# Three stretches reordered in a two-block transformer kernel: a gate unit's tiles, attention scores behind two tiles, and decays ahead of convolution terms

## The chip, the cores and the metric

The kernel runs on one core of a Trainium2 chip. Its engines work side by side, each through its own list of instructions in order: PE (TensorE, matrix products), ACT (ScalarE, functions of one operand and copies), DVE (VectorE, everything with two operands), POOL (GpSimd) and SP (SyncE, which here only starts transfers). They wait for each other by semaphores: an instruction adds to one when it is done, another waits until it has reached a value. The metric is the time of one execution on the device in microseconds (us), the median of several runs.

## The reference, cut to what matters

512 positions of 1024 float32 values go through two blocks.

```python
# first block
u = rmsnorm(h, ...); q, k, v, f, gate = split(u @ w_in_a)
h = h + (fox_attention(q, k, v, log_sigmoid(f)) * silu(gate)) @ w_out_a   # "first attention"
k_s, v_s = split(rmsnorm(h, kv_norm_g) @ w_kv)
q, gate = split(rmsnorm(h, norm_b_g) @ w_in_b)                            # 16 heads, 8 pairs
o = swa_sink_attention(rope(rmsnorm(q)), rope(rmsnorm(k_s)), v_s, sinks)  # window of 128
h = h + (o * silu(gate)) @ w_out_b                                        # "second attention"
# second block
(hq, hf, hi, hg, sq, sk, sv, iq, ik, iw, cu) = split(modulated_norm(x) @ w_in)
o_a = hgrn2_mixer(hq, hf, hi, hg)      # 4 heads: q * decays * k, chunks of 64, a state carried on
o_b = dsa_mixer(sq, sk, sv, iq, ik, iw)  # index scores pick 128 keys of each row, then softmax
o_c = conv_module(cu)                    # gated, causal depthwise filter of 31 taps, layer norm, silu
x = x + g1 * (concat([o_a, o_b, o_c]) @ w_out)
x = x + g2 * (square(relu(modulated_norm(x) @ mlp_w1)) @ mlp_w2)
return rmsnorm(x)
```

## The kernel before, in words

Everything is held transposed, features on the 128 partitions and the 512 positions along the row. A weight matrix is cut into units of 128 output columns. A unit comes in as 128 x 1024 float32 (`load_unit`), ACT rounds it to `wH` (L1936) and DVE or POOL subtracts that for the rest `wL` (L2442, L498). The product of a unit is 8 tiles of 128 input features with three matmuls each, L868 (high x high), L869 (high weight x low data) and L870 (low weight x high data), 24 matmuls of 128x512 into one bank `G`. They are `gemm(...)`, and a call may be given only some of the tiles, with other PE work in between. `FIRST` is tiles 0 to 3 and `SECOND` tiles 4 to 7. So the order in which PE works is written out by hand, in the block under `@block.tensor`, and so are those of ACT, DVE, POOL and SP.

Around the change there are three places.

**Second attention.** The loop over `n` (8 pairs of heads) interleaves, on PE, the query unit of pair n + 1 (`gemm_q`), the gate unit of pair n (`gemm_z`), scores in two halves (`scores_b(pe, n, 0)` and `(n, 1)`, L1214, L1216 and L1222, into the banks `S`), the turning of the exponentials (`turn_b`, L1269) and their product with the values (`mix_b`, L1285). `scores_b(n, 1)` writes over the banks from which ACT takes the exponentials of the first half (`exps_b`, L1249), so it waits for them. On ACT the second half of the sigmoid of the gate (`silu_scalar_2`, L887) waits for DVE (`silu_vector_1`, L882), and `take_turned_b` (L1277) and `widen_b` (L1296) feed `mix_b` and `spread_b` on PE.

**Selected attention.** DVE picks the keys with 16 rounds of MAX8 (L2758) and MATCH_REPLACE8 (L2759) for each block of rows, and between two rounds does other work (`between`), such as `logits_c` (L1115). PE meanwhile works off the input units of the second block (`gemm_i(n)`, unit UI + n) and six turns of scores (`scores_c(pe, k)`, L1103), which need queries and keys from unit 10 (`raw(10)` on ACT, L2141).

**The four heads of the recurrent mixer.** `window(t)` stands once on each engine, for head t of 0 to 3. PE makes the sums of logarithms (`diff(t, j)`, L1691) into two banks `S` in turn, ACT raises them (`decay(t, e)`, L2242, with e = j + 1), DVE multiplies them onto q and k (`operand`, L2793), PE multiplies these (`product`, L1709) and DVE gathers the results (`joined`, L2804). `diff(t, LV0 + 3)`, `LV0 + 4` and `LV0 + 5` each wait for a `joined` of DVE, because `half_of` puts products into the same banks. In windows 0 and 1 ACT also makes the terms of the depthwise filter (`conv_terms(slot)`, two terms, L2159, each into one of three buffers), and POOL adds them up (L533). A term waits until its buffer has been added. In windows 2 and 3 `conv_terms` does nothing.

Of the kernel before, what the change touches and what calls it, by code (L numbers as in the profile page):

```python
# [21 lines left out]
KT = D // P  # L22
# [146 lines left out]
def build(nc, a, out):  # L169
# [5 lines left out]
    with ctx:  # L175
# [52 lines left out]
        zraw, th = sb("zraw", [P, SEQ]), sb("th", [P, SEQ])  # L228
# [656 lines left out]
        def silu_scalar_2(act, ph, n, th):  # L885
            act.wait_ge(sem(f"{ph}_logsig"), n + 1 + since(f"{ph}_logsig"))
            s.activation(th, th, ACT.Exp).then_inc(sem(f"{ph}_sigmoid"), 1)  # L887
# [206 lines left out]
        def scores_c(pe, k):  # L1094
            t, r = C_TURNS[k]
            pe.wait_ge(sem("i_raw"), 11 + 2 * t)
            pe.wait_ge(sem("i_acc"), 24)
            for i, (q, at, w) in enumerate(A_ROUND[r]):
                for h in range(2):
                    if i == 0 and k:  # L1100
                        pe.wait_ge(sem("a_logits"), 64 + C_DONE[k - 1] + (h + 1) * (C_DONE[k] - C_DONE[k - 1]) // 2)
                    lo, hi = h * DH, (h + 1) * DH
                    last = mm(S[h][:, at:at + w], sqT[lo:hi, t, q * P:(q + 1) * P], skT[lo:hi, t, 0:w], start=(i == 0),  # L1103
                              stop=(i == len(A_ROUND[r]) - 1))
                    if i == len(A_ROUND[r]) - 1:
                        last.then_inc(sem("a_scores"), 1)
# [290 lines left out]
        def _(pe):  # L1397
# [157 lines left out]
            def gemm_z(n, part):  # L1555
                free = mark("b_raw", 1) if n == 0 else mark("b_raw", 8) if n == 7 else mark("b_zraw", n)
                gemm(pe, unit_z(n), hi2, lo2, free, part=part)
# [18 lines left out]
            for n in range(8):  # L1576
                if 0 < n < 7:
                    gemm_q(n + 1, FIRST)
                if n == 7:
                    gemm_z(n, range(2))  # L1580
                scores_b(pe, n, 0)
                if n:
                    turn_b(pe, n - 1, 1, 0)
                    turn_b(pe, n - 1, 1, 1)
                if 0 < n < 7:
                    gemm_q(n + 1, SECOND)
                if n == 7:
                    gemm_z(n, range(2, 6))
                if n:
                    mix_b(pe, n - 1, 1)  # L1590
                    spread_b(pe, n - 1)
                gemm_z(n, range(6, KT) if n == 7 else FIRST)
                scores_b(pe, n, 1)
                turn_b(pe, n, 0, 0)
                if n < 7:
                    sums_q(pe, n + 1)
                turn_b(pe, n, 0, 1)
                if n < 7:
                    gemm_z(n, SECOND)
                else:  # L1600
                    output_b(0, range(4))
                mix_b(pe, n, 0)
                if n < 7:
                    turn_q(pe, n + 1)
# [27 lines left out]
            def gemm_i(n, part=range(KT)):  # L1632
                gemm(pe, Unit(UI, n), hi2, lo2, mark("i_raw", n - 1), part=part)
# [221 lines left out]
            turn_sv(0)  # L1855
            turn_sv(1)
            gemm_i(10)
            scores_c(pe, 0)
            gemm_i(11)
            turn_c(pe, 0)  # L1860
            scores_c(pe, 1)
            gemm_i(12)
# [66 lines left out]
        def _(act):  # L1929
# [159 lines left out]
            for n in range(8):  # L2089
                if n:  # L2090
                    split_b(2 * n)
                    if n < 7:
                        silu_scalar_2(act, "b", n - 1, th[:, :])
                    take_turned_b(act, n - 1, 1)
                    widen_b(act, n - 1)
                    if n == 7:
                        silu_scalar_2(act, "b", n - 1, th[:, :])
                exps_b(act, n, 0)
                if 0 < n < 7:
                    take_q(act, n + 1)  # L2100
                if n:
                    gated_high(act, "b", n - 1, hi1)
                if n:
                    split_b(2 * n + 1)
                take_turned_b(act, n, 0)
                if n < 7:
                    root_scalar_q(act, link, n + 1)
                exps_b(act, n, 1)
                take_z(act, link, n)
# [187 lines left out]
            def take_hv(t):  # L2297
                act.wait_ge(sem("h_vturn"), t + 1 + since("h_vturn"))
                wait(act, sem("h_o"), t + since("h_o"))
                s.activation(vp[:, :, :], T[0][:, :].rearrange("p (c k) -> p c k", c=4), ACT.Copy).then_inc(sem("h_v"), 1)  # L2300
# [4 lines left out]
            def window(t):  # L2305
                def conv_terms(slot):
                    if t < 2 and 8 * t + slot < len(CONV_W) - 1:
                        terms(CONV_W[8 * t + slot], CONV_W[8 * t + slot + 1])
# [35 lines left out]
                if t == 2:  # L2344
                    act.wait_ge(sem("conv_sqsum"), 1)
                    rsqrt_scalar(link, 1, 1.0 / 256, sem("conv_var"), sem("conv_root"))
                conv_terms(2)
                decay(t, 5)
                take_hv(t)
                if t in (1, 3):  # L2350
                    root_h(t - 1)
                conv_terms(3)
# [733 lines left out]
```

## Time and profile before

| | |
|---|---|
| median of 3 runs | 1264.42 us (1263.88 to 1265.47) |
| the profiled execution | 1263.24 us, its span 1261.3 us |
| PE busy | 1247.8 us, 99% of the span |
| DVE, ACT, POOL busy | 696.7, 672.0, 370.9 us |
| mean granted TensorE clock | 0.997 |
| second attention's loop | from 375 us to 532 us |
| units of the second block's input and selected attention | from 580 us to 704 us |
| windows 0 to 3 | from 704 us to 855 us |

The span runs from the first instruction to the last; the time of the execution is 1.9 us longer. In the rows below a line of a timeline is: start, length, engine, line of the code, operation, output and inputs, shapes, how many merged into one, and in brackets how long the engine had been idle before it and what ended that. Engines overlap the end of one instruction with the start of the next, so lengths can add up to more than the distance of two starts.

### The profile page before, as it was taken

Reading aid. Unit: us, or ns where it says so; the run is one execution under the profiler, and the core shown is the slowest. Engines: PE = TensorE matmul, PEld = TensorE weight load, DVE = VectorE, ACT = ScalarE, POOL = GpSimd, SP = SyncE. Lnnn points to the kernel's source line nnn. Section 1 sums busy time; section 2 is a strip of 40 time slices with the busy share of each in tenths; the row PEclk is TensorE's granted clock in tenths of the full one; section 3 lists DMA queues with packets and bytes.
Section 4 is the critical chain, followed back from the end, with each engine's and each line's share of the span. In section 5 each row is a group of like instructions: output and inputs, shape, how many; then the busy total and the mean of one; then the engine's idle time right before and its main releaser. Section 6 shows DMA issues by size and latency. Waiting matters only on the chain.

```text
span 1261.3 us, 19235 instructions
## 1 busy us (share of the span) xinstructions
PE 1247.8 (99%) x7202; PEld 1004.7 (80%) x7202; DVE 696.7 (55%) x1477; ACT 672.0 (53%) x1278; POOL 370.9 (29%) x191
## 2 busy tenths in 40 slices
PE   9999999999999999999999999999999999999998
PEld 8777777778877777789676888888988888888887
DVE  6766667675575666565799546584662121121223
ACT  6666666666437676735667886753532242231331
POOL 0000000003410000053497784122255344353450
PEclk9999999999999999999999999999999999999999
DMA  5322243442333322252222022331363233232232
GB/s 197 112 68 84 84 145 123 134 135 96 105 101 101 101 84 85 84 176 84 84 85 71 29 70 68 118 134 47 105 217 116 70 115 101 84 107 94 84 100 68
DMA packets 38411, 128.11 MB, mean 102 GB/s; under 512 B 4640, under 2 KB 7584, under 8 KB 38320
## 3 DMA queue, kind: packets, MB, share of 16 engines
q1 hardware_dynamic: 35792, 121.91, 30.0%
q10 hardware_dynamic: 2528, 4.98, 1.2%
q8 instruction: 58, 0.95, 0.3%
q14 instruction: 33, 0.27, 0.1%
HBM read 123.43 MB, written 2.13 MB: 100 GB/s over the span
## 4 chain that ended last, share of the span: by engine, by line
PE 90%; issue 4%; DVE 2%; ACT 2%; POOL 1%; DMA 1%; ACTq 0%; DVEq 0%; POOLq 0%
PE G L868 21%; PE G L870 20%; PE G L869 20%; PE S L1691 2%; PE S L995 2%; PE O L1056 2%; PE T L1035 1%; PE S L1222 1%; PE T L1269 1%; PE O L1285 1%; PE S L1709 1%; PE N L1305 1%; PE N L1078 1%; PE N L1400 1%; PE N L1331 1%
## 5 line engine op out<-in xcount | busy, mean ns | idle before, releaser
L498 POOL TENSOR_TENSOR wL<-w,wH 128x1024 fp32r<-128x1024 f32 x119 | 290.9, 2449 | 833.9 <-ACT wH L1936 833.9
L868 PE MATMUL G<-hi,wH 128*128 128x512 f32 x1208 | 489.3, 405 | 0.8 <-DVE xT L963 0.4
L870 PE MATMUL G<-hi,wL 128*128 128x512 f32 x1208 | 472.0, 391 | 0.0
L869 PE MATMUL G<-lo,wH 128*128 128x512 f32 x1208 | 471.5, 390 | 0.0
L868 PEld LDWEIGHTS G<-hi,wH 128*128 128x128 f32 x1208 | 227.3, 188 | 58.0 <-issue 11.4
L1936 ACT ACTIVATE wH<-w 128x1024 fp32r<-128x1024 f32 x170 | 179.1, 1054 | 173.2 <-PE G L870 112.0
L870 PEld LDWEIGHTS G<-hi,wL 128*128 128x128 f32 x1208 | 227.0, 188 | 49.5
L869 PEld LDWEIGHTS G<-lo,wH 128*128 128x128 f32 x1208 | 227.7, 188 | 46.4 <-issue 3.1
L965 DVE SCALAR_TENSOR_TENSOR xT<-G,modT,xT 128x512 f32<-128x512 f32 x34 | 25.5, 751 | 124.5 <-PE G L870 124.4
L2414 ACT ACTIVATE tmp<-G 128x512 f32<-128x512 f32 x31 | 18.5, 598 | 118.4 <-PE G L870 114.8
L2442 DVE TENSOR_TENSOR wL<-w,wH 128x1024 fp32r<-128x1024 f32 x51 | 62.3, 1222 | 28.9 <-ACT wH L1936 28.0
L2965 DVE TENSOR_TENSOR T<-tmp,G 128x512 f32<-128x512 f32 x31 | 21.5, 695 | 94.4 <-ACT tmp L2414 94.4
L985 DVE CUSTOM_DVE_ANT_0 adaw<-adaw,scr 128x1024 f32<-128x1024 f32 x31 | 52.5, 1694 | 0.5 <-issue 0.4
L1023 ACT ACTIVATE scr<-scr,sa 128x256 f32<-128x256 f32 (+2 forms) x64 | 35.2, 557 | 26.9 <-DVE sa L1010 26.9
L2969 DVE TENSOR_TENSOR lo<-T,hi 128x512 fp32r<-128x512 f32 x32 | 22.1, 691 | 27.4 <-ACT hi L2421 27.4
L1249 ACT ACTIVATE scr<-S,bs,bq 128x128 f32<-128x128 f32 (+1 forms) x64 | 33.4, 536 | 3.6 <-DVE bs L1239 3.6
L2793 DVE TENSOR_TENSOR kd<-S,qkv 128x512 f32<-128x512 f32 x24 | 16.5, 689 | 30.3 <-ACT S L2242 27.7
L1046 ACT ACTIVATE scr<-T 128x384 f32<-128x384 f32 (+1 forms) x48 | 22.7, 525 | 12.0 <-PE T L1035 11.5
L1010 DVE CUSTOM_DVE_ANT_0 scr<-S,kd 128x256 f32<-128x256 f32 (+2 forms) x64 | 28.6, 487 | 0.0
L533 POOL TENSOR_TENSOR tmp<-tmp,rms 128x482 f32<-128x482 f32 (+19 forms) x20 | 24.4, 1220 | 11.2 <-ACT rms L2159 11.2
L2758 DVE MAX8 best<-adaw 128x8 f32<-128x256 f32 (+2 forms) x48 | 26.7, 557 | 0.8
L2759 DVE MATCH_REPLACE8 adaw<-best,adaw 128x256 f32<-128x256 f32 (+2 forms) x48 | 26.0, 543 | 0.0
(459 smaller groups left out, 1919.6 us busy)
## 6 DMA issues: line engine op xcount, KB each, us to landing
w<-weights_dram SPq DMA_DIRECT2D x170, 512.0 KB, 3.5
adaw<-ada_dram SPq DMA_DIRECT2D x43, 512.0 KB, 4.3
kd<-c_dram ACTq DMA_DIRECT2D x8, 512.0 KB, 3.7
cbias<-ada_dram SPq DMA_DIRECT2D x5, 512.0 KB, 4.5
xT<-x_dram SPq DMA_DIRECT2D x4, 512.0 KB, 7.9
out_dram<-xT SPq DMA_DIRECT2D x8, 256.0 KB, 2.6
scr<-ca_dram SPq DMA_DIRECT2D x2, 512.0 KB, 4.8
kd<-cbias SPq DMA_DIRECT2D x8, 128.0 KB, 3.2
```

The costliest lines, as they stand in the source:

```text
L498: g.tensor_tensor(wL[:, u.slot], w32[:, u.slot % 2], wH[:, u.slot].bitcast(f32), ALU.subtract).then_inc(w_lo, 1)
L868: mm(home[:, :], whi, H[:, k, :], start=(k == first), stop=False)
L869: mm(home[:, :], whi, L[:, k, :], start=False, stop=False)
L870: last = mm(home[:, :], wlo, H[:, k, :], start=False, stop=(k == final))
L985: v.tensor_tensor_reduce(out=home, in0=home, in1=copy, scale=1.0, scalar=0.0, op0=ALU.mult, op1=ALU.add, accum_out=modsum[:, b.n:b.n + 1]) ...
L1010: v.tensor_tensor_reduce(out=slot[:, h * 512 + at:h * 512 + at + w], in0=S[h][:, at:at + w], in1=kd[:, n % 2 * 2 + h, 0:w], scale=-1.0, sc ...
L1023: s.activation(part, part, ACT.Exp, bias=sa[:, n % 2, LOW, h, q:q + 1], scale=-1.0, accum_out=sa[:, n % 2, ASUM, h, q:q + 1]).then_inc(sem ...
L1249: s.activation(pb[:, h * 512 + at:h * 512 + at + w], S[h][:, at:at + w], ACT.Exp, bias=st[:, NEGM, h, q:q + 1], scale=bq[:, n % 2, ROOT, h ...
L1936: s.activation(wH[:, u.slot], w32[:, u.slot % 2], ACT.Copy).then_inc(w_hi, 1)
L2442: v.tensor_tensor(wL[:, u.slot], w32[:, u.slot % 2], wH[:, u.slot].bitcast(f32), ALU.subtract).then_inc(w_lo, 1)
L2758: link(v.max(best[:, n % 2, :], part))
L2759: link(v.match_replace(part, best[:, n % 2, :], part, -HUGE))
```

## The change

Four edits, all of them order. On PE, the first gate unit of the second attention (n = 0) is done as six tiles, the scores' second half, and then two tiles, where it was four and four. On PE, two of the eight tiles of unit 11 go ahead of `scores_c(pe, 0)`. On ACT, for n = 1 to 6, `silu_scalar_2` of the gate stands behind `take_turned_b` and `widen_b`, where it stood ahead of them. On ACT, in each window, `decay(t, 5)` and `take_hv(t)` stand ahead of `conv_terms(2)`.

```diff
@@ PE, second attention
-                gemm_z(n, range(6, KT) if n == 7 else FIRST)
+                gemm_z(n, range(6, KT) if n == 7 else range(6) if n == 0 else FIRST)
                 scores_b(pe, n, 1)
                 turn_b(pe, n, 0, 0)
                 if n < 7:
                     sums_q(pe, n + 1)
                 turn_b(pe, n, 0, 1)
                 if n < 7:
-                    gemm_z(n, SECOND)
+                    gemm_z(n, SECOND if n else range(6, KT))
@@ PE, selected attention
             gemm_i(10)
+            gemm_i(11, range(2))
             scores_c(pe, 0)
-            gemm_i(11)
+            gemm_i(11, range(2, KT))
             turn_c(pe, 0)
@@ ACT, second attention
                     split_b(2 * n)
-                    if n < 7:
-                        silu_scalar_2(act, "b", n - 1, th[:, :])
                     take_turned_b(act, n - 1, 1)
                     widen_b(act, n - 1)
-                    if n == 7:
-                        silu_scalar_2(act, "b", n - 1, th[:, :])
+                    silu_scalar_2(act, "b", n - 1, th[:, :])
@@ ACT, window(t)
-                conv_terms(2)
                 decay(t, 5)
                 take_hv(t)
+                conv_terms(2)
                 if t in (1, 3):
                     root_h(t - 1)
```

On PE at the first pair of the second attention the difference begins so (L1216 and L1222 are `scores_b(pe, 0, 1)`):

```order
 L869 MATMUL G<-lo,wH 128x512
 L870 MATMUL G<-hi,wL 128x512
+L868 MATMUL G<-hi,wH 128x512
+L869 MATMUL G<-lo,wH 128x512
+L870 MATMUL G<-hi,wL 128x512
+L868 MATMUL G<-hi,wH 128x512
+L869 MATMUL G<-lo,wH 128x512
+L870 MATMUL G<-hi,wL 128x512
 L1216 MATMUL S<-band,identb 128x512 x2
 L1222 MATMUL S<-kd,qkv 128x256 x4
```

Two tiles, six matmuls, moved ahead of the scores; the same six are missing behind `turn_b(pe, 0, 0, 1)`.

On PE at the first scores of the selected attention (L1103 is `scores_c(pe, 0)`):

```order
 L869 MATMUL G<-lo,wH 128x512
 L870 MATMUL G<-hi,wL 128x512
+L868 MATMUL G<-hi,wH 128x512
+L869 MATMUL G<-lo,wH 128x512
+L870 MATMUL G<-hi,wL 128x512
+L868 MATMUL G<-hi,wH 128x512
+L869 MATMUL G<-lo,wH 128x512
+L870 MATMUL G<-hi,wL 128x512
 L1103 MATMUL S<-kd,cbias 128x256 x2
 L1103 MATMUL S<-kd,cbias 128x128 x2
```

Here too six matmuls moved ahead, two tiles of unit 11.

On ACT in window 1, before (L2159 are the filter's terms, the first L2242 `decay(1, 4)`, the second `decay(1, 5)`, L2300 `take_hv(1)`, L576 the first of `root_h(0)`):

```order
L2242 ACTIVATE S<-S 128x512
L2290 ACTIVATE scr<-T 128x384
L2248 ACTIVATE vraw<-G 128x512
L2295 ACTIVATE scr<-S 64x256
L2159 ACTIVATE sq<-scr,vecT 128x507
L2159 ACTIVATE rms<-scr,vecT 128x507
L2242 ACTIVATE S<-S 128x512
L2300 ACTIVATE qkv<-T 128x512
L576 ACTIVATE rinv<-N,epsc 128x512
```

and in the change, where the lines below the edit in the second attention have numbers lower by two:

```order
L2240 ACTIVATE S<-S 128x512
L2288 ACTIVATE scr<-T 128x384
L2246 ACTIVATE vraw<-G 128x512
L2293 ACTIVATE scr<-S 64x256
L2240 ACTIVATE S<-S 128x512
L2298 ACTIVATE qkv<-T 128x512
L2157 ACTIVATE sq<-scr,vecT 128x507
L2157 ACTIVATE rms<-scr,vecT 128x507
L576 ACTIVATE rinv<-N,epsc 128x512
```

The two terms moved from ahead of `decay(1, 5)` to behind `take_hv(1)`, ahead of `root_h(0)`. In window 0 it is the same with the terms of 499 elements, and no `root_h` stands there.

## Rows read from the trace of the kernel before

**Rows 1.** The page, part 1: busy time, share of the span, instructions of each engine.
```profile
PE 1247.8 (99%) x7202; PEld 1004.7 (80%) x7202; DVE 696.7 (55%) x1477; ACT 672.0 (53%) x1278; POOL 370.9 (29%) x191
```

**Rows 2.** The waits of PE, whole span: us in total, times, longest.
```profile
PE N L1400 <- DVE epsc L2446: 1.1, 1, 1.1
```

**Rows 3.** The timeline of the second attention's first pair, PE and ACT.
```profile
378.07 0.39 PE L870 MATMUL G<-hi,wL 128*128 128x512 f32 x1
...
378.75 0.39 PE L870 MATMUL G<-hi,wL 128*128 128x512 f32 x1
...
380.04 0.59 PE L1216 MATMUL S<-band,identb 128*128 128x512 bf16 x2 [0.90 <-ACT scr L1249]
...
383.38 0.49 ACT L1277 ACTIVATE scr<-T 128x384 f32<-128x384 f32 x1 [0.68 <-PE T L1269]
...
386.03 0.88 PE L1285 MATMUL O<-scr,vb 128*64 128x128 f32 x12
```

**Rows 4.** The timeline of ACT and DVE in pair 2 of the second attention.
```profile
412.91 0.63 ACT L887 ACTIVATE th<-th 128x512 f32<-128x512 f32 x1 [1.89 <-DVE th L882]
...
418.10 0.69 DVE L1365 TENSOR_TENSOR scr<-qraw,cs 128x512 f32<-128x512 f32 x1 [2.00 <-ACT qraw L1340]
```

**Rows 5.** The timeline of PE at the first scores of the selected attention.
```profile
646.17 0.39 PE L870 MATMUL G<-hi,wL 128*128 128x512 f32 x1
647.24 0.92 PE L1103 MATMUL S<-kd,cbias 64*128 64x256 f32 x8 [0.69 <-ACT kd L2141]
```

**Rows 6.** The timeline of ACT and DVE at the fifth turn of that attention.
```profile
690.95 0.71 ACT L1127 ACTIVATE scr<-scr,sa 128x512 f32<-128x512 f32 x1
...
690.15 0.69 DVE L1115 CUSTOM_DVE_ANT_0 scr<-S,adaw 128x512 f32<-128x512 f32 x1
```

**Rows 7.** The timeline of window 0: ACT, DVE, PE.
```profile
713.73 0.71 ACT L2159 ACTIVATE sq<-scr,vecT 128x499 f32<-128x499 f32 x1 [0.73 <-POOL tmp L533]
...
717.52 0.58 ACT L2242 ACTIVATE S<-S 128x512 f32<-128x512 f32 x1
...
721.09 0.58 ACT L2242 ACTIVATE S<-S 128x512 f32<-128x512 f32 x1
...
722.32 0.45 DVE L2804 COPY_PREDICATED scr<-level,S 128x256 f32<-128x256 uint8 x1
...
716.07 1.16 PE L1691 MATMUL S<-adaw,scr 128*128 128x128 f32 x8 [0.68 <-DVE scr L2804]
...
723.03 1.05 PE L1691 MATMUL S<-turnm,scr 128*128 128x128 f32 x8
```

**Rows 8.** The timeline of POOL in window 0.
```profile
714.68 1.24 POOL L533 TENSOR_TENSOR tmp<-tmp,rinv 128x499 f32<-128x499 f32 x1
```

**Rows 9.** The timeline of window 1: ACT, DVE, PE.
```profile
743.88 0.71 ACT L2159 ACTIVATE sq<-scr,vecT 128x507 f32<-128x507 f32 x1
744.49 0.70 ACT L2159 ACTIVATE rms<-scr,vecT 128x507 f32<-128x507 f32 x1
747.46 0.58 ACT L2242 ACTIVATE S<-S 128x512 f32<-128x512 f32 x1 [2.26 <-PE S L1691]
...
748.75 0.69 ACT L576 ACTIVATE rinv<-N,epsc 128x512 f32<-128x512 f32 x1 [0.21 <-PE N L1756]
...
753.42 0.57 ACT L2242 ACTIVATE S<-S 128x512 f32<-128x512 f32 x1
...
761.22 0.44 DVE L2804 COPY_PREDICATED scr<-level,S 128x256 f32<-128x256 uint8 x1
...
761.71 1.16 PE L1691 MATMUL S<-turnm,scr 128*128 128x128 f32 x8
```

**Rows 10.** Busy time of stretches: us, PE, PEld, DVE, ACT, POOL, PEclk, DMA share, GB/s.
```profile
737.70:741.70 4.00, 4.00 (x24) 3.42 (x24) 3.87 (x5) 4.00 (x7) 2.87 (x2) 1.00 0.01 2
...
821.10:824.20 3.10, 3.04 (x26) 2.82 (x24) 3.10 (x4) 1.02 (x2) 2.00 (x1) 1.00 0.01 3
824.50:828.50 4.00, 4.00 (x12) 3.09 (x12) 4.00 (x8) 1.61 (x3) 0.05 (x1) 0.57 0.27 73
```

## Prediction

> **What bounds the kernel now.** I read part 1 of the page first: PE is busy for 1247.8 of the span's 1261.3 us, 99%, and the next engine, DVE, for 55% [rows 1]. So the time is PE's work plus the moments in which PE stands still, and a change of order can only win or lose such moments. The list of PE's waits came next: it has 13 rows of one or two waits each, 7.7 us in all, and the longest is 1.1 [rows 2]. Three of them lie where the change puts its hands: 0.90 us before the second half of the first pair's scores [rows 3], 0.69 before the first scores of the selected attention [rows 5], 0.68 in window 0 [rows 7]. They add up to 2.27 us, 0.18% of the time. Everything after was a reading of timelines around these three and of what stands behind them. The chain of waits says only that PE ends last, which part 1 says too.
>
> A change under 0.2%, 2.5 us, is about what a measurement of this kernel cannot tell from no change; all chances below use that bound.
>
> **The first gate unit of the second attention.** PE ends its fourth tile and stands 0.90 us until ACT has taken the exponentials out of the banks [rows 3]. By starts, from 378.75 to 380.04 are 1.29 us, where one matmul follows the last in 0.23 (from 378.07 to 378.75 are three), so up to 1.06 go. Two tiles more are six matmuls, 6 x 0.23 = 1.37 us, longer than that gap. The scores then start at 378.75 + 0.23 + 1.37 = 380.35, no longer for ACT's sake, and 0.31 later than before. What comes after has two tiles less in it, so `mix_b(0, 0)` comes 1.06 earlier, at 384.97 instead of 386.03. It waits for ACT's second `take_turned_b`, which started 383.38, took 0.49 and now shifts by those 0.31, to an end at 384.18 [rows 3]: 0.8 us to spare. Gain: 0.90 by the recorded wait, 1.06 by the starts; I take 1.06, because the same reading of starts is what PE loses. Bounds: 0, if the 0.8 to spare and ACT's lateness below eat it, and 1.06.
>
> The pair's `take_z` and its followers on ACT come 0.31 later by the clock while PE is 1.06 earlier, so ACT is 1.37 nearer to being late. That is where the third edit helps.
>
> **The sigmoid behind the turned tiles (n = 1 to 6).** ACT stood 1.89 us before L887 for DVE [rows 4], and everything behind it in ACT's queue, the two `take_turned_b` and `widen_b`, stood with it. Now those go first. PE waits nowhere in these pairs in steady state, so nothing is won. What is late instead is `silu_vector_2` on DVE, by the length of what was moved ahead of it less the idle time saved, below 1 us; behind it on DVE stands one `ada_block` and then 2.00 us of idle time until L1365 [rows 4], which takes it. Cost 0, with that idle time as its cover; if it were gone, the next exponentials would be up to 1 us later, once. No term.
>
> **Two tiles ahead of the index stage's scores.** PE stood 0.69 us for the copy of keys [rows 5]. Start to start it is 1.07 us where one matmul follows a tile in 0.23 to 0.32, so 0.75 to 0.84 are open (0.69 by the recorded wait) and 1.37 us of tiles cover it. The scores start 646.17 + 0.23 + 1.37 + 0.1 = 647.87, 0.6 later than now, and their reader on DVE sits between two rounds of the key search and is not waiting for them. PE is then 0.75 earlier through this attention, while DVE, which works its rounds without a break, is not. So I looked for the place where DVE's rounds and PE meet. It is the fifth turn: DVE begins the second head's logits at 690.15 [rows 6], so the first head's are done just then, and ACT begins its exponentials at 690.95 without having waited. 0.75 earlier is 690.20. It just fits; I count 0.05 as lost. The step is worth 0.70, with bounds 0 (DVE decides after all) and 0.84.
>
> **Decays ahead of terms, window 0.** PE stood 0.68 us for a `joined` of DVE [rows 7], which hung on `decay(0, 5)`, which stood behind a filter term that had itself waited 0.73 us for POOL [rows 7]. With the decay first, that wait goes, all 0.68. But the two terms are only moved behind it. POOL adds without a break here, and the add that frees the buffer of the second term of 500 elements ends at 714.68 + 1.24 = 715.92 [rows 8]. So that term can't start before 715.92, which is where it starts already, and `split_h(4)`, `decay(0, 6)` at 717.52, the gate's three functions, two more terms and `decay(0, 7)` at 721.09 [rows 7] stay where they are: ACT is full from there on. DVE's `joined` after `decay(0, 7)` still ends at 722.32 + 0.45 = 722.77, and PE needs it for the row at 723.03. PE would now come to it at 722.35 and can start at some 722.85. Of the 0.68, 0.2 is left. Bounds: 0 and 0.68.
>
> **Decays ahead of terms, window 1.** Here the same edit costs. Before, ACT made the two terms at 743.88 and 744.49, 0.61 apart, 1.2 us in all, inside a stretch in which it then stood idle for 2.26 us more until PE's sums for `decay(1, 5)` were there [rows 9]. That decay does not come earlier, it waits for PE. The terms now come behind it and behind `take_hv(1)`, at some 748.45, where ACT had 0.3 us of waiting left before `root_h(0)` [rows 9]; so `root_h(0)`, two terms, a split and `decay(1, 6)` come 1.2 - 0.3 = 0.9 later, at 754.3 instead of 753.42. DVE goes on from that decay without idle time: operand, `joined`, the norm of head 0, states, operand, and the `joined` that begins at 761.22 and ends at 761.66. PE's row at 761.71 starts 0.05 behind it [rows 9]: it has no slack at all. Its length of 1.16 us is that of the row at 716.07 which had waited, against 1.05 for the row at 723.03 which had not [rows 7], a second sign that PE was already waiting for it a little. So PE waits 0.9 us more, once. Bounds: 0 (something in DVE's chain shrinks by as much) and 1.2 (both terms in full). I take 0.9. In windows 2 and 3 there are no terms and nothing moves.
>
> **The sum.** -1.06 - 0.70 - 0.20 + 0.90 = -1.06 us, so the profiled execution's 1263.24 (its span of 1261.3 and 1.9 around it, which the change doesn't touch) would be 1262.2. That execution lies 1.2 us below the median of the runs shown, so the median to be expected is 1264.42 - 1.06 = 1263.4, 0.08% less.
>
> **The clock.** In the stretch from 824.5 to 828.5 the granted clock is 0.57 on average, that is mostly the lower level of 1.2 GHz instead of 2.4. What PE did just before it were 26 pieces of small matmuls of `outputs` [rows 10], after sums of 128 columns. The fall costs 4.00 x 0.43 = 1.7 us, as much as any two of the terms above. Behind the same small matmuls of window 1 it stayed at 1.00 [rows 10], so the order of the work alone does not decide it. The Trainium skill, page "TensorE: Matmul & The Clock Gate", section "Part 1: The HAM clock gate (the "warmup" mystery)", says that the monitor runs freely and is not reset when a kernel starts. By that rule the change would neither remove nor add falls on average, the sum stays -1.06, and the runs scatter by a fall; if instead PE's order fixed it, the sum would be -2.8 or +0.6. No run here shows which.
>
> **The rivals.**
> - The window 1 price isn't paid, or window 0 keeps its whole gain. For: DVE's norm in window 1 runs beside POOL, and a chain that is stretched by another engine may shrink when it is moved. Against: the `joined` of 761.22 leads PE's row by nothing [rows 9]. Without the 0.9 it is -1.96, 1262.5; with the 0.68 in full as well, -2.44, 1262.0, and with 1.06, 0.84 and 0.68 all taken it is 1261.8, just over the bound.
> - A gain is taken back, the wait moved from PE's first scores to its later turns, because DVE's rounds pace the selected attention. For: ACT meets DVE at the fifth turn with nothing to spare [rows 6]. Against: the meeting is at the very end of the 0.75. Then +0.70 on the sum: -0.36, 1264.1.
> - Slower: one more fall of the clock behind one of the four stretches of small matmuls, whose starts all shift against whatever decides a fall. It costs 1.7 [rows 10]. With the sum it is +0.6, 1265.1. It outweighs the gain from the first additional fall on; to be slower by over 0.2% two more falls with window 1 at its full 1.2 would be needed, +2.6. For: one of the four stretches fell. Against: the three runs lie within 1.6 us, less than one fall, so their number hardly varied.
> - The change moves nothing that counts, 1264.4: ACT's later start after the first gate unit could hand the 1.06 back at the next pair. Against: 0.8 us to spare there [rows 3].
>
> **How the numbers follow.** The forecast 0.50, the first rival 0.20 (a third of which beyond the bound), the second 0.12, the additional fall 0.12, nothing 0.06. The likeliest gives 1263.4. The range goes from 1261.7 (all three waits gone, nothing paid) to 1265.0 (an additional fall), which leaves some 0.15 outside, with the scatter of a median of few runs, 0.8 to each side, in it. Faster by over 0.2% is below 1261.9: a third of the first rival, and as much again if a median happens to hold one fall less, 0.13. Slower by over 0.2% is above 1266.95, 0.02. The rest, 0.85, is no change to be told.
>
> **What the profile of the changed kernel would show.** If the steps are right, the waits of L1216 and L1103 are gone from PE's list; the L1691 of window 0 that waited at 716 no longer does, but the second one after it waits 0.3 to 0.5; and a wait of L1691 for DVE's `joined` of about 0.9 us is new, in window 1, with `decay(1, 6)` that much later against `decay(1, 5)`. I am wrong in window 1 if that wait is not there, and wrong in the index stage if the waits of L1140 for ACT have grown by 0.7 together. I am wrong in the whole if PE's busy time has changed by more than a fall of the clock explains.

## The result, and the profile after

| | before | after |
|---|---|---|
| median of 6 runs each | 1264.15 us (1263.46 to 1265.92) | 1269.26 us (1268.93 to 1270.57) |
| ratio, 95% interval | | 1.0036 (1.0026 to 1.0046) |
| the profiled execution, its span | 1263.24, 1261.3 us | 1269.26, 1267.5 us |
| PE, DVE, ACT, POOL busy | [rows 1] | 1252.4, 698.2, 671.9, 370.6 us |
| mean granted TensorE clock | 0.997 | 0.996 |

The change makes the kernel 0.36% slower, 5 us by the medians (6.0 between the two profiled executions, of which before's lies 0.9 below its median). The forecast was 0.08% faster and "no change to be told" with a chance of 0.85. It was wrong.

PE's list of waits in the kernel after (engine, line, waited for, us in total, times, longest) answers to [rows 2]:

```profile
PE S L1103 <- DVE sa L1115: 2.0, 1, 2.0
PE S L1691 <- DVE scr L2802: 2.0, 4, 0.7
PE N L1400 <- DVE epsc L2444: 1.1, 1, 1.1
PE T L1421 <- DVE vraw L1203: 1.0, 1, 1.0
...
PE T L1140 <- ACT scr L1127: 0.8, 2, 0.5
```

The waits of L1216 for ACT (0.90) and of L1103 for the copy of keys (0.69) are gone, as forecast. At the head stands one that no row of before resembles: L1103 waited 2.0 us for DVE's L1115. Below it, L1691's one wait of 0.68 has become four.

I lined up the starts of PE's matmuls in both traces, the same instruction with the same, and read how far the kernel after is behind. It is 0.53 us behind before the second attention (a difference that arises in the kernel's first 12 us, far from the change), and then:

| place (by the clock of after) | PE gains (-) or loses (+), us | what the trace has there |
|---|---|---|
| 386, first pair | -1.02 | no wait of L1216 |
| 647, first scores | -0.74, in two steps | no wait of L1103 for the keys |
| 692, fifth turn of scores | +2.04 | wait of L1103 for DVE's L1115 |
| 693 to 697 | +1.71 | granted clock 0.50, the lower level of 1.2 GHz |
| 718 to 728, window 0 | -0.94 + 0.82 + 0.47 | one wait of L1691 gone, two new |
| 741 to 747 | +1.58 | granted clock 0.50 |
| 767, window 1 | +0.87 | wait of L1691 for DVE's `joined` |
| 785 to 792 | +1.68 | granted clock 0.50 |
| 825 to 830 | -1.55 | granted clock 0.50 in before, 1.00 in after |
| 855, window 3 | +0.78 | wait of L1691 for DVE's `joined` |

Shifts of at most 0.4 us are left out; they are -0.14 at 567, +0.33 at 598 (of which below) and -0.26 together behind 1036.

The first four rows are 1.99 us lost where the forecast had 1.76 won. What happened at the fifth turn stands in the timeline of DVE, ACT, PE and POOL of the kernel after:

```profile
680.89 2.36 POOL L498 TENSOR_TENSOR wL<-w,wH 128x1024 fp32r<-128x1024 f32 x1 [4.30 <-ACT wH L1937]
...
681.40 2.40 DVE L882 SCALAR_TENSOR_TENSOR kraw<-qraw,kraw 128x512 f32<-128x512 f32 x1
...
688.27 2.92 POOL L498 TENSOR_TENSOR wL<-w,wH 128x1024 fp32r<-128x1024 f32 x1 [0.96 <-ACT wH L1937]
...
690.38 1.10 DVE L2760 TENSOR_SCALAR adaw<-adaw 128x512 f32<-128x512 f32 x1
691.52 0.69 DVE L1115 CUSTOM_DVE_ANT_0 scr<-S,adaw 128x512 f32<-128x512 f32 x1
...
692.25 0.72 ACT L1127 ACTIVATE scr<-scr,sa 128x512 f32<-128x512 f32 x1 [2.26 <-DVE sa L1115]
...
692.36 2.33 PE L1103 MATMUL S<-kd,cbias 64*128 64x512 f32 x4 [1.98 <-DVE sa L1115]
```

and in the same timeline of the kernel before, whose later rows are [rows 6]:

```profile
681.75 0.69 DVE L882 SCALAR_TENSOR_TENSOR kraw<-qraw,kraw 128x512 f32<-128x512 f32 x1
...
681.95 2.72 POOL L498 TENSOR_TENSOR wL<-w,wH 128x1024 fp32r<-128x1024 f32 x1 [4.31 <-ACT wH L1936]
...
689.06 0.43 DVE L2762 TENSOR_SCALAR adaw<-adaw 128x512 f32<-128x512 f32 x1
...
689.34 2.42 POOL L498 TENSOR_TENSOR wL<-w,wH 128x1024 fp32r<-128x1024 f32 x1 [0.60 <-ACT wH L1936]
```

The reader is to see the order of two starts, twice. Before, DVE's L882 (`queries_1(0)`, between rounds 11 and 12 of the last key search) began 0.20 us ahead of POOL's L498 and took 0.69; POOL's instruction was the one that was stretched, to 2.72. After, PE and with it ACT and POOL are a little over a microsecond earlier, DVE only 0.35, and POOL begins 0.51 ahead. Now L882 takes 2.40 and ends 0.55 behind POOL's end (680.89 + 2.36 = 683.25). The same again at the search's last instruction, the TENSOR_SCALAR: 0.28 ahead of POOL before, 2.11 behind its start after, and 1.10 instead of 0.43. -0.35 + 1.71 + 0.67 = 2.03 us is how much later L1115 starts (1.99 by its rows).

### The profile page after: what moved, and what is told of

It is laid out like the page before. It is cut to its first block, busy times and chain, and to the rows that moved or that the text cites. A ratio compares the mean times of both kernels' runs of the same rounds, so it can differ in the third digit from the quotient of the medians.

```text
span 1267.5 us, 19235 instructions
## 1 busy us (share of the span) xinstructions
PE 1252.4 (99%) x7202; PEld 1007.0 (79%) x7202; DVE 698.2 (55%) x1477; ACT 671.9 (53%) x1278; POOL 370.6 (29%) x191
## 4 chain that ended last, share of the span: by engine, by line
PE 86%; issue 5%; ACT 3%; DVE 3%; DMA 1%; POOL 1%; ACTq 0%; DVEq 0%; POOLq 0%
PE G L868 20%; PE G L869 19%; PE G L870 19%; PE S L995 2%; PE O L1056 2%; PE T L1035 1%; PE S L1691 1%; PE S L1222 1%; PE T L1269 1%; PE O L1285 1%; ACT wH L1937 1%; PE N L1400 1%; POOL tmp L533 1%; PE N L1305 1%; PE N L1078 1%
## 5 line engine op out<-in xcount | busy, mean ns | idle before, releaser
L498 POOL TENSOR_TENSOR wL<-w,wH 128x1024 fp32r<-128x1024 f32 x119 | 290.4, 2445 | 834.9 <-ACT wH L1937 834.9
L1277 ACT ACTIVATE scr<-T 128x384 f32<-128x384 f32 (+1 forms) x32 | 16.4, 544 | 25.0 <-PE T L1269 25.0
L1046 ACT ACTIVATE scr<-T 128x384 f32<-128x384 f32 (+1 forms) x48 | 22.7, 525 | 11.9 <-PE T L1035 11.4
```

Source lines behind the costliest of these rows:

```text
L498: g.tensor_tensor(wL[:, u.slot], w32[:, u.slot % 2], wH[:, u.slot].bitcast(f32), ALU.subtract).then_inc(w_lo, 1)
```

## The experiments

My theory after this reading: the two tiles ahead of `scores_c(0)` turn a gain of 0.74 into a loss, by way of DVE instructions that start just behind POOL's L498; the decays' order in window 1 costs its forecast 0.9; falls of the clock add to both. Rival 1: falls come with any shift of PE's order and are the whole loss. Rival 2: the decays' order carries most of it. Rival 3: DVE's rounds pace the selected attention, without anything being stretched. In the diffs, - is the kernel named and + the experiment.

**The parts alone.** e1_A is the first gate unit and the sigmoid's place, e2_B the two tiles, e3_C the decays, e4_AC the change without the two tiles; each is the change's own diff for that part, applied to the kernel before.

> The kernel before with the first gate unit split into a part of six tiles and a part of two (and the silu order that goes with it), and nothing else. Theory (the two tiles' shift ahead of scores_c(0) set off the new stall, and C adds to it): TensorE gains the 1.02 us that the trace after shows at this place and no wait of L1103 on DVE's L1115 appears: 1263.1 us, ratio 0.9992 (0.9985 to 0.9998). Rival 1 (the additional clock falls come by themselves with any shift of TensorE's order): one or two falls more, 1264.8 to 1266.5, ratio above 1.0004. Rival 2 (the decays' order carries most of the loss): the same 0.9992 here, so this run does not speak on it.

> The kernel before with only the two tiles of unit 11 put ahead of scores_c(0). Theory: the start of TensorE's first scores gains 0.74, but DVE's L882 (queries_1(0)) falls beside POOL's L498 and takes about 2.4 instead of 0.69 us, DVE's L1115 ends about 2 later, L1103 waits about 2.0 on it, and a clock fall of about 1.7 follows: +1.3 to +3.0, 1265.4 to 1267.1, ratio 1.0010 to 1.0024. Rival 2 (the decays' order carries the loss): -0.7 or nothing, ratio 0.9994 to 1.0000. Rival 3 (the selected attention is paced by DVE's rounds, no collision): +0 to +0.4, and L882 stays at 0.7.

> The kernel before with only the decays' order of windows 0 and 1 changed. Theory: window 1 loses 0.87 (L1691 waits 0.7 for DVE's joined state) and window 0 about 0.3 net, so +0.9 to +1.2 without additional clock falls: 1265.0 to 1265.4, ratio 1.0007 to 1.0010; with a fall more 1.0022. Rival 2 (the decays' order carries most of the loss): +3 to +5, ratio above 1.0024. Rival 1 (clock falls alone): one or two more falls, +1.7 to +3.4, with L1691's waits no longer than before.

> The changed kernel without the two tiles ahead of scores_c(0) (the gate split, and the decays' order in windows 0 and 1). Theory: -1.0 from the split and +0.9 to +1.2 from the decays, and neither the wait of 2.0 on DVE's L1115 nor its clock fall: 1264.0 to 1264.5, ratio 0.9999 to 1.0003; 1.0016 if a fall comes with the decays. Rival 1 (clock falls by phase): 1265.7 to 1267.4. Rival 2 (the decays carry most): 1267 to 1269, ratio above 1.002.

| | ratio, 95% interval | PE's new waits in its trace |
|---|---|---|
| e1_A | 0.9995 (0.9986 to 1.0004) | L1629 for a DMA, 0.5; window 3's |
| e2_B | 1.0017 (1.0009 to 1.0026) | L1103 for L1115, 2.0; window 3's |
| e3_C | 1.0016 (1.0006 to 1.0025) | L1691, four of 2.0 together, window 3's among them |
| e4_AC | 1.0009 (1.0000 to 1.0018) | L1691, three of 1.5 together |

The two tiles alone are slower, the decays alone too. e2_B's timeline of DVE and PE repeats that of the kernel after:

```profile
681.86 2.40 DVE L882 SCALAR_TENSOR_TENSOR kraw<-qraw,kraw 128x512 f32<-128x512 f32 x1
...
690.84 1.10 DVE L2763 TENSOR_SCALAR adaw<-adaw 128x512 f32<-128x512 f32 x1
...
692.83 1.69 PE L1103 MATMUL S<-kd,cbias 64*128 64x512 f32 x4 [1.98 <-DVE sa L1115]
```

Rival 2 falls as the whole story, rival 3 on the 2.40 (L882 would have stayed at 0.7). Rival 1 as "any shift" falls on e1_A, whose interval ends at 1.0004 though it had a fall at 738 in its trace. e4_AC came out above the 0.9999 to 1.0003 expected, which its interval still reaches; its trace had one fall more than that of before.

In e1_A's trace PE gains 1.03 at the first pair, as in after, and gives 0.45 back at 598, where L1629 waits for a copy by DMA that has not landed (timeline of PE):

```profile
598.53 0.48 PE L1629 MATMUL S<-qraw,cs 32*128 32x256 f32 x2 [0.53 <-DMA qraw<-vraw]
```

This wait stands in twelve of the sixteen traces, with 0.21 to 0.56 us: in all seven that have the gate unit's edit (0.45 on average) and in five of the nine others (0.18 on average over the nine; none in before). So the landing differs from one execution to the next, but a PE that comes earlier waits for it longer.

**Whose duration is it?** e5_B_q10 is e2_B with L882 one round earlier. e6_late_q leaves PE's order as it was before and puts L882 half a round later.

```diff
-                elif n == 11:          # e5_B_q10, against e2_B
+                elif n == 10:
                     queries_1(0)
```
```diff
-                elif n == 11:          # e6_late_q, against the kernel before
-                    queries_1(0)
...
                     link(v.max(best[:, n % 2, :], part))
+                    if q == 3 and n == 12:
+                        queries_1(0)
                     link(v.match_replace(part, best[:, n % 2, :], part, -HUGE))
```

> The kernel of e2_B (two tiles of unit 11 ahead of scores_c(0)), with DVE's L882 (queries_1(0)) moved one of DVE's rounds earlier, so that it stands ahead of POOL's L498 and not behind its start. Theory (the two operations beside each other cost 1.7 on DVE's one operation, then the wait of 2.0): L882 takes 0.7 again, the wait of L1103 on DVE's L1115 and its clock fall go, the gain of 0.74 stays: about 1263.8, ratio 0.9994 (0.9988 to 1.0000). Rival 3 (no collision: DVE's rounds simply pace the selected attention): DVE has the same amount of work before L1115, so the wait stays, ratio 1.0010 to 1.0017 as e2_B's 1.0017.

> The kernel before, TensorE's order untouched, with DVE's L882 (queries_1(0)) moved back by half a round of DVE (about 0.7 us), so that POOL's L498 is under way when it starts. Theory: L882 takes about 2.4 instead of 0.7, L1115 ends about 2 later and L1103 waits 2.0 less the 0.74 that TensorE isn't early here, about 1.3, with a clock fall behind it or not: ratio 1.0010 to 1.0024. Rival 3 (TensorE's earlier arrival alone makes the wait): no wait, ratio 0.9997 to 1.0003. Rival 1 (falls alone): no wait, and a fall or none.

e6_late_q: 1.0019 (1.0011 to 1.0028), with this timeline of POOL, DVE and PE:

```profile
682.55 2.36 POOL L498 TENSOR_TENSOR wL<-w,wH 128x1024 fp32r<-128x1024 f32 x1 [4.30 <-ACT wH L1936]
...
683.06 2.40 DVE L882 SCALAR_TENSOR_TENSOR kraw<-qraw,kraw 128x512 f32<-128x512 f32 x1
...
691.32 1.31 DVE L2762 TENSOR_SCALAR adaw<-adaw 128x512 f32<-128x512 f32 x1
...
693.51 1.65 PE L1103 MATMUL S<-kd,cbias 64*128 64x512 f32 x4 [1.47 <-DVE sa L1115]
```

No tile was moved, no instruction added, and one DVE instruction stands 0.7 us later: the kernel is as slow as with the two tiles. With the starts of PE's matmuls lined up against before, this trace loses 2.05 us at the fifth turn (after and e2_B 2.04). So the loss at that place is made without moving PE, by the order of the two starts alone. The TENSOR_SCALAR too was stretched here, to 1.31.

e5_B_q10: 1.0010 (1.0001 to 1.0019), where I had expected 0.9994. The timeline of DVE, POOL and PE:

```profile
682.37 0.69 DVE L882 SCALAR_TENSOR_TENSOR kraw<-qraw,kraw 128x512 f32<-128x512 f32 x1
...
683.29 2.36 POOL L498 TENSOR_TENSOR wL<-w,wH 128x1024 fp32r<-128x1024 f32 x1 [4.30 <-ACT wH L1937]
...
690.71 2.41 POOL L498 TENSOR_TENSOR wL<-w,wH 128x1024 fp32r<-128x1024 f32 x1 [1.45 <-ACT wH L1937]
...
691.24 2.17 DVE L2763 TENSOR_SCALAR adaw<-adaw 128x512 f32<-128x512 f32 x1
...
694.29 1.65 PE L1103 MATMUL S<-kd,cbias 64*128 64x512 f32 x4 [1.47 <-DVE sa L1115]
```

PE loses 2.09 at the fifth turn. L882 has its 0.69 back, but the TENSOR_SCALAR now starts 0.53 behind POOL's second L498 and takes 2.17 instead of 0.43. I had cured one of two meetings. That the wait stays fits rival 3 as well, and only the duration of 2.17 speaks against it.

**Both meetings taken away.** Both instructions on the head's queries leave the search, for a place where DVE idles; the Exp between them moves on ACT accordingly. e10_B_qout has this on top of e2_B, e11_AB_qout on top of e1_A and e2_B together, e12_qout on the kernel before.

```diff
-                elif n == 11:                 # DVE, between the rounds
-                    queries_1(0)
-                elif n == 14:
-                    queries_2(0)
...
             logits_c(dve, 5)                  # DVE, after the search
+            queries_1(0)
...
             shares_c(dve, 1)
+            queries_2(0)
...
                 take_turned_c(act, 3)         # ACT
-                silu_scalar_2(act, "hq", 0, kraw[:, :])
...
                 raw_h(0, 3, zraw, sem("sv_turned"), 2)
+                silu_scalar_2(act, "hq", 0, kraw[:, :])
```

> The kernel of e2_B (two tiles of unit 11 ahead of scores_c(0)), with both of DVE's hq operations (L882 and L2713) taken out of the key search and put behind logits_c(5), where DVE idles; the Exp on ACT between them goes behind raw_h(0, 3). Theory (whichever of DVE's operations starts just behind POOL's L498 is stretched until that ends; in e5_B_q10 it was the TENSOR_SCALAR L2763, 2.17 instead of 0.43): the TENSOR_SCALAR starts 1.3 us further ahead and is done before POOL's second L498 starts, takes 0.43, L1103 waits for nothing, and the 0.74 stays gained: ratio 0.9994 (0.9986 to 1.0002). Rival 3 (the search's rounds pace it and TensorE's earlier arrival is lost in any case): the same kernel has 1.3 less DVE work ahead of L1115, so it gives this too if no operation were stretched; the two part in e12_qout and in the durations, not in this ratio. Rival 1 (falls by phase): 1.0010 or more with no wait of L1103 on L1115.

> A candidate to beat both: e10_B_qout with the split gate unit, the decays' order as before. Theory: -1.02 and -0.74 where they arise, 1.8 us in all less what e1_A gave back (its ratio was 0.9995, half of its 1.02): ratio 0.9988 (0.9980 to 0.9996). Rival 1 (falls by phase): 0.9995 to 1.0010.

> The kernel before, TensorE's order untouched, with the two hq operations out of the key search as in e10_B_qout. Theory: no wait of TensorE depended on them in the kernel before, DVE's TENSOR_SCALAR keeps its 0.43, so nothing changes: ratio 1.0000 (0.9993 to 1.0007). If this gains as much as e10_B_qout, then e10_B_qout's gain isn't that of the two tiles.

| | ratio, 95% interval |
|---|---|
| e10_B_qout | 0.9990 (0.9981 to 0.9999) |
| e11_AB_qout | 0.9987 (0.9977 to 0.9996) |
| e12_qout | 0.9994 (0.9985 to 1.0003) |

e10_B_qout's timeline of DVE, POOL and PE:

```profile
688.20 0.43 DVE L2759 TENSOR_SCALAR adaw<-adaw 128x512 f32<-128x512 f32 x1
...
689.07 2.41 POOL L498 TENSOR_TENSOR wL<-w,wH 128x1024 fp32r<-128x1024 f32 x1 [1.44 <-ACT wH L1937]
...
691.11 1.13 PE L1103 MATMUL S<-kd,cbias 64*128 64x512 f32 x4
...
693.51 0.72 DVE L882 SCALAR_TENSOR_TENSOR kraw<-qraw,kraw 128x512 f32<-128x512 f32 x1
```

The same two tiles that made the kernel 0.17% slower are in a kernel that is 0.10% faster. e12_qout, expected at 1.0000, can't be told from that, and not from e10_B_qout either: by the times, how much of e10's gain is the two tiles' stays open. The traces say more. Lined up against before, e10 gains 0.74 at the first scores and loses nothing from there to 824; e12 stays where it was, within 0.05, until a fall at 780. So the two tiles' 0.74 is kept in full once the meetings are gone. e11_AB_qout, median 1263.09 us against 1264.60 for the kernel before on the same chip, has the lowest ratio of all and is faster than the kernel before.

**The decays by window.** The same diff, in window 0 only (e7_C0) and in window 1 only (e9_C1), written shorter here.

```diff
-                conv_terms(2)
+                if t != 0: conv_terms(2)      # e9_C1: t != 1
                 decay(t, 5)
                 take_hv(t)
+                if t == 0: conv_terms(2)      # e9_C1: t == 1
```

> The kernel before with the decays' order changed in window 0 only. Theory: the first wait of L1691 (0.68) goes and two of 0.5 and 0.2 come, with POOL's add of 1.69 ahead of them, as the trace after has it: -0.94 + 0.82 + 0.36 = +0.3, ratio 1.0002 (0.9998 to 1.0007, the upper end with some additional falls). The forecast on record had -0.2. If most of e3_C's 1.0016 is in window 1, this one stays below 1.0007; if it is above 1.0010, window 0 or the falls that it sets off carry it.

> The kernel before with the decays' order changed in window 1 only. Theory: L1691 waits about 0.7 for DVE's joined state and TensorE loses the 0.87 that the trace after shows there: ratio 1.0007 (1.0002 to 1.0014 with the falls' chance). With e7_C0's 1.0004 that makes e3_C's 1.0016 but for a fall. If window 1 costs nothing by itself, the ratio is 1.0000 and e3_C's loss is that of falls.

e7_C0: 1.0004 (0.9995 to 1.0012). e9_C1: 1.0017 (1.0007 to 1.0026). So e3_C's loss is that of window 1, where the trace of e9_C1 (timeline of DVE and PE) has

```profile
762.29 0.44 DVE L2807 COPY_PREDICATED scr<-level,S 128x256 f32<-128x256 uint8 x1
...
762.78 1.16 PE L1691 MATMUL S<-turnm,scr 128*128 128x128 f32 x8 [0.72 <-DVE scr L2807]
```

PE loses 0.87 there, 0.07%; the ratio says more, and its interval begins just where that ends. The profiled execution was the shortest of the eleven, so what the others lost besides is in no trace. Their mean granted clock, 0.9965 against 0.9968 for before beside them, accounts for some 0.4 us of it (an estimate, 0.0003 of 1265 us).

**A candidate that missed.** e8_ABqC0 is both first parts with e5's order on DVE and the decays in window 0.

> A candidate: the split gate unit, the two tiles ahead of scores_c(0) with L882 one round earlier, and the decays' order changed in window 0 only. Theory: -0.5 to -1.0 (e1_A), -0.74, +0.3: -1.0 to -1.4, 1263.1 to 1263.5, ratio 0.9989 to 0.9992. Rival 3: +1.3 to +2 in place of the -0.74, ratio 1.0006 to 1.0014. Rival 1 (falls by phase): anything between 1.0000 and 1.0020, with more falls than the one in the trace before and no wait of L1103 on L1115.

It had 1.0005 (0.9996 to 1.0014) where 0.9989 to 0.9992 was expected, and for e5's reason: the TENSOR_SCALAR began 0.58 behind POOL's start and took 2.11, L1103 waited 1.5, and PE lost 2.04 at the fifth turn.

**The whole change with the meetings taken out.** e13_after_qout is the kernel after with the diff of e10_B_qout; e14_ABC0_qout also has the decays' order in window 0 only.

> The whole changed kernel, with both hq operations out of the key search. Theory (the stretched operations behind the two tiles, and window 1's decays, are the two causes): L882 and the TENSOR_SCALAR keep 0.7 and 0.43, no wait of L1103 on L1115, no clock fall near 694; what is left is e11_AB_qout's 0.9987 times e3_C's 1.0016, so 1.0003 (0.9995 to 1.0012), 1263.6 to 1265.8. If part of the loss comes of the three edits together (their single ratios multiply to 1.0028, the whole has 1.0036) by something else than these two, this stays at 1.0015 or more. Rival 1 (falls by phase): 1.0015 or more with two or three falls and none of the two waits.

> As e13_after_qout, with the decays' order changed in window 0 only. Theory: window 1's 0.87 and the falls that came with it (e9_C1's 1.0017) go: e11_AB_qout's 0.9987 times e7_C0's 1.0004, 0.9991 (0.9983 to 0.9999). If window 1's order is no cause, the same as e13_after_qout.

e13_after_qout: 1.0000 (0.9991 to 1.0010). e14_ABC0_qout: 0.9991 (0.9980 to 1.0001), as expected but not to be told from e13. Window 1's 0.86 is still paid in e13's trace. With two DVE instructions at another place the change costs nothing that can be measured, where it cost 0.36%; e12_qout's ratio allows up to 0.15% of that to be the move's own. In e13's trace the TENSOR_SCALAR has its 0.43 and L1103 waits for nothing; PE's stretch of the fifth turn, which in the kernel after lay in the fall of the clock, has the full clock (columns as in [rows 10], first e13_after_qout):

```profile
690.00:696.00 6.00, 5.66 (x33) 3.91 (x34) 3.22 (x11) 4.18 (x12) 4.05 (x4) 1.00 0.28 87
```

and the kernel after, the three falls:

```profile
693.20:696.61 3.41, 3.41 (x12) 1.69 (x10) 1.39 (x6) 1.17 (x3) 1.38 (x2) 0.50 0.27 103
740.98:744.40 3.42, 3.42 (x9) 2.64 (x10) 3.29 (x5) 3.15 (x6) 2.29 (x2) 0.50 0.00 0
785.36:788.77 3.41, 3.41 (x6) 1.68 (x5) 1.34 (x2) 0.17 (x1) 0.19 (x1) 0.50 0.50 154
```

## Why the prediction was wrong, point by point

- **First gate unit, -1.06.** Right where it arises: 1.02 in the trace of after, 1.03 in that of e1_A. What the forecast didn't look for is the copy by DMA that L1629 waits for at 598: there 0.33 of it goes again in after and 0.45 in e1_A. The run of it alone, 0.9995, can't be told from no change.
- **The sigmoid's place, 0.** Right. No wait of PE appeared in these pairs, and L1365's idle time, the cover named, shrank from 2.00 to 1.35 us.
- **Two tiles ahead of the scores, -0.70.** This is the step that failed. The 0.74 arose where it should. The failing sentence is "It just fits; I count 0.05 as lost", and behind it "DVE, which works its rounds without a break": I moved PE against DVE by 0.75 and let every DVE instruction keep its length. ACT and POOL move with PE, and DVE's two plain instructions that began 0.20 and 0.28 us ahead of POOL's L498 came to stand behind its start. The term should have been -0.74 + 2.04 = +1.30, and in this trace a fall stands behind it. I had looked at the rounds and at [rows 6] only, never at POOL's row beside L882, though its 2.72 us against 2.42 in the next one showed that two instructions met there.
- **Window 0, -0.20.** The mechanism was right in part (one wait goes and comes back later), size and sign not: +0.35. Two waits came, 0.54 at the next row of sums, which the forecast didn't have, and 0.20 at the one after it, for which it had 0.3 to 0.5. "That term can't start before 715.92" took POOL's add of 1.24 [rows 8] as fixed; in the kernel after the add of that term took 1.69. DVE's L1196 had begun behind the start of the add ahead of it, ended 0.55 behind that add's end, and the add that frees the buffer stood behind L1196:

```profile
716.35 1.06 POOL L533 TENSOR_TENSOR tmp<-tmp,rms 128x498 f32<-128x498 f32 x1
...
717.05 0.91 DVE L1196 TENSOR_TENSOR lo<-sg,hi 128x512 fp32r<-128x512 f32 x1
717.37 1.69 POOL L533 TENSOR_TENSOR tmp<-tmp,rinv 128x499 f32<-128x499 f32 x1
...
719.10 0.71 ACT L2157 ACTIVATE rinv<-scr,vecT 128x500 f32<-128x500 f32 x1 [0.73 <-POOL tmp L533]
...
722.39 1.16 PE L1691 MATMUL S<-pair,scr 128*128 128x128 f32 x8 [0.54 <-DVE scr L2802]
...
725.95 1.16 PE L1691 MATMUL S<-turnm,scr 128*128 128x128 f32 x8 [0.20 <-DVE scr L2802]
```

  The rows are of the kernel after's timeline of DVE, POOL, ACT and PE. Up to here its adds are 2.70 us later by the clock than those of before (716.35 against 713.65); the term of 500 elements, in before at 715.96, is 3.14 later. So the add cost 0.44, `decay(0, 6)` and `decay(0, 7)` came that much later than foreseen, and so did each `joined` behind them. In the kernel before the same L1196 met the next add (timeline of POOL and DVE), and no term at 715.96 had to wait for it:

```profile
715.89 1.24 POOL L533 TENSOR_TENSOR tmp<-tmp,sq 128x499 f32<-128x499 f32 x1
...
715.91 1.77 DVE L1196 TENSOR_TENSOR lo<-sg,hi 128x512 fp32r<-128x512 f32 x1
```

  It is the same kind of meeting of DVE and POOL, a third time. In the time of a run, e7_C0's 1.0004, it can't be told from nothing.
- **Window 1, +0.90.** Right in place, sign and size: 0.87 in the trace, answering to [rows 9]:

```profile
766.70 0.43 DVE L2802 COPY_PREDICATED scr<-level,S 128x256 f32<-128x256 uint8 x1
...
767.19 1.16 PE L1691 MATMUL S<-turnm,scr 128*128 128x128 f32 x8 [0.72 <-DVE scr L2802]
```

- **The clock.** I gave one fall the price of 1.7 us [rows 10]; the three of after took 1.71, 1.58 and 1.68. Forecast was that their number stays. It didn't: the mean granted clock went from 0.9969 (124 runs of before beside the experiments) to 0.9952 (6 runs of after). Three falls in one trace came behind different work: PE was busy 2.22 of the 4.2 us before the one at 693, in which L1103 waited, and 3.94 of the 4.0 us before those at 741 and 785, with short matmuls of 64 and 128 columns. The change in the mean is 0.0017 of 1265 us, 2.1 us or somewhat more than one fall. As an estimate, 2 of the 5 us that the change costs are falls and 3 are order and waits. The Trainium skill, page "TensorE: Matmul & The Clock Gate", section "Part 1: The HAM clock gate (the "warmup" mystery)", has the monitor run freely; where falls stood in the sixteen traces doesn't speak against that: at 571 in one, about 694 in two, 736 to 745 in seven, 780 to 789 in six, 823 to 832 in six and 857 to 868 in ten: a few places, and another choice of them in each trace. Only the place at 694 goes with something: it fell in the two traces in which L1103 waited 2.0 us and in none of the other fourteen. That a wait sets off a fall is suggested by this, not shown: e5_B_q10, e6_late_q and e8_ABqC0 lost the same 2.04 to 2.09 us at that turn, in a wait of 1.5 and a rest among the four matmuls behind it, and had no fall there. (Beyond these places all sixteen have a fall in the last few us of the kernel, from 1258 on.)
- **The rivals.** The second ("DVE's rounds pace the selected attention") had the right place, with +0.70 for its price and no thought of stretched instructions; the third had the right sign, by falls alone.
- **The signs.** L1140's waits for ACT, my sign for the index stage, stayed at 0.8. The wait came to L1103 instead, which hangs on DVE's L1115 directly, where L1140 hangs on it by way of ACT's L1127: a sign has to name every consumer of what may be late.

The sum of the trace: -1.02 - 0.74 + 2.04 + 0.35 + 0.87 is +1.50 for order and waits, the three falls are +4.97, and the fall that only before had, with the wait in window 3, is -1.55 + 0.78 = -0.77. Together 5.70, and with the 0.53 of the kernel's first 12 us 6.2, the difference of the two spans; the small shifts left out add up to less than 0.1.

## What to carry to other kernels

When one engine is shifted against another by less than a microsecond, look for every pair of DVE and POOL instructions whose starts lie closer than the shift, and ask which starts first after it; each such pair can turn from free to a full POOL instruction of delay on DVE. A search or another unbroken chain on DVE should hold only instructions that POOL does not stretch; the others go where DVE idles. And a fix that frees one such meeting has to be followed along the chain to the next.

## What the runs showed of the hardware

**Which DVE instructions POOL stretches.** Beside POOL's L498 (two inputs and an output in SBUF, 2.36 to 2.41 us where it isn't held up here) these were stretched when they began behind it: L882, SCALAR_TENSOR_TENSOR with two SBUF inputs, 0.69 to 2.40, ending 0.55 us behind POOL's end in after, e2_B and e6_late_q alike; and the TENSOR_SCALAR with one input, which alone takes 0.43 for 512 columns where the others take 0.69, to 1.10, 1.31, 2.11 and 2.17, ending 0.29 behind POOL's end in e5_B_q10 (691.24 + 2.17 against 690.71 + 2.41). Not stretched were the rounds of the search, whose instructions take 512 columns of one input in 0.68 (timeline of DVE, e5_B_q10, where L498 ran from 683.29 to 685.65):

```profile
683.78 0.68 DVE L2760 MATCH_REPLACE8 adaw<-best,adaw 128x512 f32<-128x512 f32 x1
```

and L1115, whose other input lies in a PSUM bank, kept 0.69 at 689.53 in the kernel before, beside L498 from 689.34 to 691.76. When DVE's instruction began first, POOL's was the longer one: 2.72 beside L882 in before, 2.92 in after beside a SCALAR_TENSOR_TENSOR with two SBUF inputs (L2710) that began 0.01 ahead of it.

The rule can be counted. In the sixteen traces there are 311 DVE instructions of 128x512 with two SBUF inputs (TENSOR_TENSOR and SCALAR_TENSOR_TENSOR) that began while a TENSOR_TENSOR of POOL had more than 0.1 us to go. Every one of them ended 0.55 to 0.58 us behind the end of POOL's. Of some 1,500 with one of the two inputs in a PSUM bank that began during one of POOL's, none took more than 0.76 us. The Trainium skill, page "SBUF — State Buffer", section "🔬 SBUF: two separate sides", says it as a rule: a DVE instruction in a two-port mode, or with two SBUF inputs against a POOL instruction that reads SBUF, and the POOL instruction exclude each other, and "whichever" of the two "starts first gets the pair for the whole instruction". Every row here agrees, with the 0.29 and 0.55 us behind POOL's end on top. That the TENSOR_SCALAR runs in such a mode is read from its 0.43 us alone. With that rule in hand the forecast's step could have been priced from [rows 6] and POOL's rows.

**What a fall of the clock hides.** Ten of the sixteen traces have a wait of L1691 for DVE of 0.51 to 0.55 us near 850, in window 3; in the kernel after (timeline of PE)

```profile
854.65 1.16 PE L1691 MATMUL S<-turnm,scr 128*128 128x128 f32 x8 [0.51 <-DVE scr L2802]
```

They are exactly the ten without a fall at 823 to 832. Where PE is slowed by 1.6 us just before, DVE has caught up and 0.8 of it comes back. So one and the same fall cost 1.55 at its place and 0.77 in the end, and a kernel profiled in one execution with such a fall shows one wait too few.
